# Sums of squares without identity products, an early Sqrt table, split dots, later small loads, and the second angles behind the first recurrences

## The reference, cut to what matters

```
mod = (silu(c) @ w_ada[layer] + b_ada[layer])            # 6 x 1024: sh1, sc1, g1, sh2, sc2, g2
hmix = rms_norm(x) * norm_mix * (1 + sc1) + sh1
proj = hmix @ w_in                                        # 1024 x 2944
att, ret, ssm = attention(...), retention(...), s5_ssm(...)
x = x + g1 * (merged(att, ret, ssm) @ w_out)
hffn = rms_norm(x) * norm_ffn * (1 + sc2) + sh2
x = x + g2 * peer(hffn)                                   # product keys, 16384 experts
return rms_norm(x) * final_norm
```

## Time and profile before

| | us |
|---|---|
| three runs | 2061.97, 2064.07, 2069.95 |
| median | 2064.07 |
| the profiled execution | 2061.11 |
| its span | 2059.3 |
| busy in the span: PE / PEld / DVE / ACT / POOL | 2009.6 / 1745.3 / 1606.0 / 1029.8 / 238.4 |

### The profile page before, as it was taken

How to read it: one execution, slowest core, us unless ns; L and a number is a source line. 1 busy time by engine, 2 the same in 40 slices (tenths; PEclk the granted TensorE clock), 3 DMA queues, 4 the chain that set the end, 5 groups by cost and what they waited for, 6 DMA issues and landing times.

```text
span 2059.3 us, 35040 instructions
## 1 busy us (share of the span) xinstructions
PE 2009.6 (98%) x11676; PEld 1745.3 (85%) x11676; DVE 1606.0 (78%) x3454; ACT 1029.8 (50%) x1675; POOL 238.4 (12%) x335
## 2 busy tenths in 40 slices
PE   5999999999999999999999999999999999999998
PEld 5899989888888888887788999998888888888877
DVE  8897999777888888887757579997766766778854
ACT  3235568655444444444522456785555555554433
POOL 2004436100000000000010053550000000000000
PEclk9999999999999999999999999999999999999999
DMA  9566842455778877556453478115555555555461
GB/s 371 176 247 229 243 129 65 156 196 204 275 284 296 300 276 278 190 183 214 147 174 112 163 217 234 65 62 207 183 186 196 208 204 205 195 185 177 176 241 54
DMA packets 119776, 406.94 MB, mean 198 GB/s; under 512 B 13200, under 2 KB 21264, under 8 KB 119184
## 3 DMA queue, kind: packets, MB, share of 16 engines
q1 hardware_dynamic: 113072, 381.77, 52.6%
q0 software_dynamic: 3744, 13.63, 3.4%
q10 hardware_dynamic: 2880, 10.49, 1.5%
HBM read 398.50 MB, written 7.34 MB: 197 GB/s over the span
## 4 chain that ended last, share of the span: by engine, by line
PE 72%; DVE 15%; ACT 4%; issue 4%; DMA 3%; SPq 1%; POOL 1%; DVEq 0%; ACTq 0%; POOLq 0%
PE ps L966 26%; PE ps L957 13%; PE ps L959 6%; PE ps L927 5%; PE ps L673 4%; DVE v_lo L1864 3%; DVE next_w_ada_ring L1913 3%; PE ps L685 2%; DVE u_lo L1859 2%; PE ps L935 2%; PE ps L872 1%; DVE gated L1872 1%; PE ps L873 1%; PE ps L874 1%; ACT gelu L1376 1%
## 5 line engine op out<-in xcount | busy, mean ns | idle before, releaser
L957 PE MATMUL ps<-h_hi_lo,u_hi 128*128 128x512 f32 x1696 | 616.6, 398 | 0.8
L959 PE MATMUL ps<-h_hi_lo,u_lo 128*128 128x256 f32 x1484 | 416.1, 280 | 0.0
L957 PEld LDWEIGHTS ps<-h_hi_lo,u_hi 128*128 128x128 f32 x1696 | 318.6, 188 | 69.5 <-DVE u_lo L1859 2.7
L959 PEld LDWEIGHTS ps<-h_hi_lo,u_lo 128*128 128x128 f32 x1484 | 280.1, 189 | 8.0
L966 PE MATMUL ps<-v_hi,gated_hi 128*128 128x512 f32 x848 | 267.2, 396 | 5.2 <-DVE gated_lo L1878 4.0
L1859 DVE TENSOR_TENSOR u_lo<-weight_ring,u_hi 128x1024 fp32r<-128x1024 f32 x212 | 259.0, 1222 | 9.4 <-ACT u_hi L1365 6.0
L966 PE MATMUL ps<-v_lo,gated_hi 128*128 128x512 f32 x848 | 263.2, 392 | 0.0
L966 PE MATMUL ps<-v_hi,gated_lo 128*128 128x512 f32 x848 | 261.4, 389 | 0.0
L1864 DVE TENSOR_TENSOR v_lo<-weight_ring,v_hi 128x1024 fp32r<-128x1024 f32 x212 | 258.5, 1219 | 0.0
L1376 ACT ACTIVATE gelu<-gelu 128x256 f32<-128x256 f32 x212 | 88.6, 418 | 337.7 <-DVE gelu L1868 337.7
L1370 ACT ACTIVATE v_hi<-weight_ring 128x1024 fp32r<-128x1024 f32 x212 | 223.2, 1053 | 50.9 <-PE ps L966 50.9
(11 more groups left out here) (343 smaller groups left out, 3502.9 us busy)
## 6 DMA issues: line engine op xcount, KB each, us to landing
weight_ring<-in_u_tab_dram SPq DMA_DIRECT2D x220, 512.0 KB, 4.3
weight_ring<-in_v_tab_dram SPq DMA_DIRECT2D x212, 512.0 KB, 3.6
next_w_ada_ring<-in_w_ada_dram SPq DMA_DIRECT2D x56, 512.0 KB, 4.5
weight_ring<-in_w_in_dram SPq DMA_DIRECT2D x46, 512.0 KB, 3.6
v_tail<-in_v_tab_dram SPq DMA_DIRECT2D x44, 512.0 KB, 3.8
w_ada_ring<-in_w_ada_dram SPq DMA_DIRECT2D x40, 512.0 KB, 8.8
weight_ring<-in_w_q_dram SPq DMA_DIRECT2D x32, 512.0 KB, 5.1
u_ahead_lo<-in_u_tab_dram POOLq DMA_DIRECT2D x26, 512.0 KB, 8.2
```

The lines of the kernel that those rows point to most:

```text
L957: last = mm(both, UH[:, b, k, :], HB[:, :, k, :], start=(k == 0), stop=(k == KT - 1))
L959: mm(PS[:, 4 + b, 0:T], UL[:, b, k, :], HH[:, k, :], start=False, stop=False)
```

## The change

It has these parts:

1. The identity products between the tiles of the sums of squares of norms 2 and 4 stay only ahead of k = 0: 14 fewer in each of the two norms.
2. ScalarE issues a Sqrt on RS at the start of norm n for n >= 1. Its result is overwritten before anybody reads it; the Sqrt table is loaded ahead of it.
3. ada(2) is cut into dots 0 to 4 at the old place and dots 5 to 7 behind the subtraction of the maxima (L1656).
4. The identity matrix is loaded behind w_ada transfers 4 to 7, the masks behind transfer 15, the final gain behind the permutation matrix and with its own semaphore. ScalarE's wait for the masks moves from ahead of norm 0 to behind shift 0.
5. ADA_BEHIND lets transfers 29 to 31 of w_ada follow tile 20 of w_in instead of tile 19.
6. VectorE's angles(0, 1, ...) move from ahead of the recurrences of u = 0 to behind them, and ScalarE evacuates projections 5 to 7 ahead of trig(0, 1, ...) instead of behind it.

```diff
-        ADA_BEHIND = [... ] + [24, 24, 24, 28, 32, 32, 32, 32, 32, 40]
+        ADA_BEHIND = [... ] + [24, 24, 24, 28, 29, 32, 32, 32, 32, 40]
...
                     sp.dma_start(X[:, :, :], xT.rearrange("(k p) t -> p k t", p=P)).then_inc(in_x, 16)
+                    for m in range(4, 8):
+                        ada(m)
                     sp.dma_start(IDENT[:, :], ident_c).then_inc(in_const, 16)
-                    sp.dma_start(FCOL[:, :], fcol).then_inc(in_small, 16)
+                    for m in range(8, 16):
+                        ada(m)
                     sp.dma_start(MASK[:, :], mask_c).then_inc(in_small, 16)
-                    for m in range(4, 16):
-                        ada(m)
...
                 if l == 0:
+                    sp.dma_start(FCOL[:, :], fcol).then_inc(in_fcol, 16)
                     sp.wait_ge(cond_done, 1)
...
-                    elif n and n % 2 == 0:
+                    elif n and n % 2 == 0 and k == 0:
                         keep_clock(n, 2)
...
             def norm(n):
+                if n:
+                    fn(RS[:, :], RS[:, :], ACT.Sqrt)
                 for k in range(KT):
...
-                    act.wait_ge(in_small, 32)
                 norm(2 * l)
                 shift(2 * l, SH1)
+                act.wait_ge(in_small, 16)
...
-                for j in range(5):
+                for j in range(8):
                     taken(j)
                 if l == 0:
                     for step in range(4):
                         trig(0, 1, step)
-                for j in range(5, 13):
+                for j in range(8, 13):
                     taken(j)
...
                     for part in range(3):
                         ssm_factors(0, part)
-                    for step in range(6):
-                        angles(0, 1, step)
                 for u in range(2):
...
                     dve.wait_ge(xs_done, 2 * l + u + 1)
+                    if l == 0 and u == 0:
+                        for step in range(6):
+                            angles(0, 1, step)
...
                 if l == 0:
-                    ada(2)
+                    ada(2, dots=range(5))
...
                                 ALU.subtract).then_inc(att_sub, 1)
+                if l == 0:
+                    ada(2, dots=range(5, 8))
...
             rms(2 * L)
+            dve.wait_ge(in_fcol, 16)
             norm(2 * L, FCOL)
```

More of the change, by code:

```diff
@@ L243, in trunk @@
         in_cols = sem("cols_loaded")
+        in_fcol = sem("final_gain_in")
         in_small = sem("gain_and_masks_loaded")
@@ L412, in trunk @@
         IN_ORDER = [21, 22, 9, 10, 11, 12, 13, 14, 0, 1, 2, 3, 4, 5, 6, 7, 8, 15, 16, 17, 18, 19, 20]
-        ADA_BEHIND = [16 + min(8, 2 * max(0, n - 3)) for n in range(15)] + [24, 24, 24, 28, 32, 32, 32, 32, 32, 40]
+        ADA_BEHIND = [16 + min(8, 2 * max(0, n - 3)) for n in range(15)] + [24, 24, 24, 28, 29, 32, 32, 32, 32, 40]
         N_PROJ = 20
@@ L1030, in _ @@
             for l in range(L):
-                pool.wait_ge(in_small, 32)
+                pool.wait_ge(in_small, 16)
                 pool.wait_ge(in_ssm, 80 * (l + 1))
@@ L1554, in ssm_factors, with ada @@
                         v.tensor_tensor(sv(14), sv(11), sv(10), ALU.mult).then_inc(f_done, 1)
-                def ada(i, between=None):
-                    for j in range(8):
+                def ada(i, between=None, dots=range(8)):
+                    for j in dots:
                         if between and j in between:
@@ L1563, in ada @@
                                                op0=ALU.mult, op1=ALU.add, accum_out=ADA8[:, j:j + 1]).then_inc(ada_used, 1)
+                    if 7 not in dots:
+                        return
                     dve.wait_ge(ada_used, (i + 1) * 8)
```

## The result

The changed kernel takes 2067.22 us, the median of 12 runs (2064.45 to 2069.59), beside 2062.71 for the kernel before, also 12 runs (2061.18 to 2069.95). The ratio is 1.0020, 95% interval [1.0011, 1.0028]: 4.5 us slower, where 3 us faster was forecast. The profiled execution has a span of 2065.2 us, 5.9 more than before.

What follows compares the result with a forecast made beforehand. The prediction put 72% of the chain of waits on TensorE, mostly untouched expert loops. Its terms, +4.9 - 1.85 - 6.0 = -2.95, gave 2058.1 us for the profiled execution and 2061 from the median; range 2054 to 2068.

Steps and rivals of the forecast that it cites:

- Part 6, +4.9: Layer 0's mixer: TensorE stands 5.0 us before ssm_output(1), waiting for the second recurrence; +4.9 us, bounds +4.2 and +5.6.
- 41.8, 43.0, 62.1, 68.0, 72.3 and 91.4: Layer 0, forecast us: ssm_input(0) starts; recurrence 0 starts, ends; angles end; trig ends; recurrence 1 ends.
- rival A: Behind the wait at ssm_output(1): idling lets TensorE's clock fall to half pace; +2.7 us, 2064; chance 0.23.
- Parts 3 and 5, -1.85: Layer 0's attention scores: made three dots sooner, so TensorE's wait goes completely; -1.85 us, bounds -1.85 and 0.
- Parts 1 and 2, -6.0: Norms 2 and 4: sums of squares end sooner and the Sqrt table load leaves the path; -3.0 us each, -6.0 together.
- rival B: Norms 2 and 4: one-column products don't hold the clock; about +3.5 and +2, total +8.6, 2073 (2075 with A); chance 0.09.
- Part 4, -0.2: The start: rms(0) +0.4 us from the later identity, but POOL's b_im_T is faster; ssm_input(0) starts 0.2 us sooner.

Runs made afterwards that it cites:

- part 6, without the pause: The kernel before with part 6 alone, without VectorE's second wait for the table of token numbers; 2068.70 us, ratio 1.0028, +6.2.

## Why the prediction was wrong

I forecast 3 us faster and the kernel came out 4.5 us slower. Two steps failed: the price of parts 1 and 2 with the clock held, and a wait instruction that I gave no price at all. Part 6 also cost somewhat more than its wait. The single parts measure +6.2 (part 6, without the pause), -3.1, -3.4 and +0.4: together +0.1, beside +0.4 for the changed kernel with one wait fewer. The pause adds about 4 in the medians of the changed kernel, and 2.1 where one wait brought it into the kernel before. Beside my terms:

- **Part 6, +4.9.** The step was right in every row: 41.35, 42.64, 61.89, 67.85, 72.13 and 91.30 against 41.8, 43.0, 62.1, 68.0, 72.3 and 91.4. What I gave as rival A came with it. "It had worked for 50 us before" was the false argument against it: the clock fell during the wait. By the medians part 6 costs 6.2, not 4.9 (interval 3.7 to 8.0). I also took the clock's 1.00 in the earlier trace rows for a reading of full pace; the trace's first record of the clock stands at 33.4 us, so that 1.00 says nothing about the start, where the products of the earlier trace rows ran at 0.22 us each.
- **Parts 3 and 5, -1.85.** Right: R is 1.9 us shorter and nothing is late next. The medians give 1.2 us more, perhaps the clock at that wait too (argued, not shown).
- **Parts 1 and 2, -6.0.** This step failed, by 2.6 us. The sum does end 3 us sooner where the clock holds to its end (-3.1 forecast), and the table is off the path. I set rival B aside because "the stretch without wide products is only 3.5 us"; yet in all ten profiles without the identity products the clock fell in or behind both sums. The price of rival B was wrong too, since mostly only the tail is slow. Over those profiles N2 runs from 6.79 to 9.09 us and N4 from 6.68 to 9.07, with means of 7.7 and 7.6, against 9.4: 1.7 us gained a norm. N2 ends ahead of part of the slow stretch, though. With one wait more it is 6.79 and the clock falls only behind it. Counted to layer 1's first recurrence, the ten gain 0.3 to 2.0 us, 1.3 on the mean, and counted from norm 4's first square to the end of the span 0.3 to 2.7, 1.8 on the mean. That is about 3 us in all, beside 3.2 and 3.4 by the medians. Rival B's +3.5 for a fall in one norm is refuted: the clock fell in both, and part 1 was still worth over 3 us.
- **Part 4, -0.2.** The identity landed at 19.89, not 20.3, and h was not delayed; TensorE's wait for POOL's mask is gone as foreseen. The median, +0.4, tells nothing against 0.
- **Not priced: a wait instruction more.** I costed each wait by whom it holds up. Part 6's costs by being there, since a loop 1.8 ms later stands one instruction further on and then lies across a load of instructions. It is probably the largest miss, about 4 us by the medians (2.1 in the kernel before) and 2.8 in the traces, and it turns a kernel equal to the one before (+0.4) into a slower one.

So the mechanisms of rivals A and B were real, at a fraction of the prices that I gave them, and with them the sum is near 0. The rest is the loop's place.

## What to carry to other kernels

A wait put in front of TensorE costs its length, and the clock can fall behind it; price both, and the same for a stretch in which TensorE gets one-column products alone. Still, such products can be worth more than the clock they lose: time the version with and without them, since half the filler here took time and still lost the clock. Read single profiles beside the mean clocks of many executions before a microsecond is put down to a cause. Where a tight loop is bound by the engine that runs it, look for idle time of the kind "issue" at its first instruction whenever the stream ahead of it has grown by even one instruction, and then in the DMA view for a packet of the instruction queue inside the loop.

## What the runs showed of the hardware

- A loop of VectorE that makes two tiles in 11.65 us paused 0.17 us at every pass when it stood one or two instructions later in the stream, 0.06 us with six, and not at all with 44. In every profile with the pause, and in no other, one packet of the instruction queue fell behind the loop's first branch and none for the rest of it (changed kernel 1857.0 us; kernel before 1970.0 us, behind the last branch).
- TensorE's clock fell to 0.50 while one-column products ran back to back, with TensorE recorded as busy for 2.00 of each 2 us; one product of 128 columns for every tile did not hold it, two did.
- How far a norm suffers differs from one profile to the next by more than 2 us (N2 6.8 to 9.1 us for the same code of the norm), since the fall starts at another point of it: 2.3 us behind the first square where N2 was 9.09, and 5.3 us behind it where N2 was 6.79.
- The mean granted clock of the same kernel differs between executions, and the time with it: 2062.1 us at 0.999 and 2065.8 us at 0.997 in the kernel before.
